# Wide product columns, turned gate rows, and a moved seam in two projection, attention and PLE stages

## The reference

```python
hn = rms_norm(h, g_mix[i])
z = hn @ w_in[i]                                   # 2840 columns
z_a, z_b, z_c = split_cols(z, (A_COLS, B_COLS, C_COLS))
y_a = chunked_spatial_gating(z_a, ...)             # 'mix': w @ layer_norm(v) + bias, times u
y_b = rwkv7_time_mix(z_b, ...)                     # a recurrence, 4 heads, 256 steps
y_c = nsa_attention(z_c, cos, sin, ...)            # three attentions, gates sigmoid(z)
h = h + jnp.concatenate([y_a, y_b, y_c], axis=-1) @ w_out[i]
h = h + (dense or expert FFN)(rms_norm(h, g_ffn[i]))
gate = jax.nn.sigmoid(rms_norm(h, g_ple[i]) @ ple_gate_w[i])
h = h + (p[i] @ ple_proj_w[i]) * gate
```

## Time and profile before

| | us |
|---|---|
| median of 3 runs | 2979.14 (2975.31 to 2981.68) |
| the profiled execution | 2979.76 |
| its span | 2978.0 |
| TensorE busy | 2824.9 (95%) |
| VectorE busy | 2056.7 (69%) |
| ScalarE busy | 1533.4 (51%) |
| projection, layer 0 | from 0.7 to 163.3 |
| attention, layer 0 | from 163.3 to 247 |
| PLE, layer 0 | from 437.9 to 478.8 |
| projection, layer 1 | from 478.9 to 629.2 |
| PLE, layer 1 | from 1568.5 to 1616.4 |

### The profile page before, as it was taken

How to read it: one execution, slowest core, us unless ns; L and a number is a source line. 1 busy time by engine, 2 the same in 40 slices (tenths; PEclk the granted TensorE clock), 3 DMA queues, 4 the chain that set the end, 5 groups by cost and what they waited for, 6 DMA issues and landing times. The chain is left out here.

```text
span 2978.0 us, 45722 instructions
## 1 busy us (share of the span) xinstructions
PE 2824.9 (95%) x17660; PEld 2382.1 (80%) x17660; DVE 2056.7 (69%) x2990; ACT 1533.4 (51%) x2398; POOL 21.4 (1%) x22
## 2 busy tenths in 40 slices
PE   8979999987999999999997999989999999989998
PEld 8847888954778777877786888979888888979887
DVE  7356764554888988898882776675576776675576
ACT  6144334233777777777773434554434434554433
POOL 0000000100000000000000000000000000000000
PEclk9999999997999999999998999999999999999999
DMA  6144543203788898898864556243554556244551
GB/s 264 48 168 147 194 154 118 97 1 134 294 330 340 333 363 331 335 366 337 339 248 183 204 194 207 80 162 145 183 193 146 204 194 203 84 160 146 184 195 38
DMA packets 102049, 599.07 MB, mean 201 GB/s; under 512 B 23166, under 2 KB 28798, under 8 KB 32780
## 3 DMA queue, kind: packets, MB, share of 16 engines
q1 hardware_dynamic: 101900, 596.99, 53.3%
HBM read 594.04 MB, written 6.12 MB: 202 GB/s over the span
## 5 line engine op out<-in xcount | busy, mean ns | idle before, releaser
L2393 DVE TENSOR_TENSOR expert_w_low<-weight_ring,expert_w_high 128x1024 fp32r<-128x1024 f32 x528 | 631.3, 1223 | 63.9 <-ACT expert_w_high L2337 53.4
L728 PE MATMUL psum<-hnT_parts,weight_high 128*128 128x512 f32 x1760 | 620.1, 394 | 0.5
L2337 ACT ACTIVATE expert_w_high<-weight_ring 128x1024 fp32r<-128x1024 f32 x528 | 555.2, 1059 | 100.4 <-PE psum L2268 56.8
L730 PE MATMUL psum<-hnT_parts,weight_low 128*128 128x256 f32 x1760 | 493.0, 280 | 0.0
L782 DVE TENSOR_TENSOR weight_low<-weight_ring,weight_high 128x1024 fp32r<-128x1024 f32 x330 | 384.8, 1219 | 12.0 <-ACT weight_high L776 12.0
L728 PEld LDWEIGHTS psum<-hnT_parts,weight_high 128*128 128x128 f32 x1760 | 330.8, 188 | 75.8 <-DVE hnT_parts L469 1.6
L730 PEld LDWEIGHTS psum<-hnT_parts,weight_low 128*128 128x128 f32 x1760 | 331.2, 188 | 3.9
L776 ACT ACTIVATE weight_high<-weight_ring 128x1024 fp32r<-128x1024 f32 x330 | 324.8, 1045 | 8.3 <-PE psum L747 8.3
L795 ACT ACTIVATE gate_act<-gate_sum 128x256 f32<-128x256 f32 x110 | 46.0, 418 | 519.5 <-DVE gate_sum L827 519.5
L2268 PE MATMUL psum<-expert_w_high,expert_x_high 128*128 128x512 f32 x704 | 288.5, 410 | 2.0 <-DVE expert_x_low L2412 1.9
L2268 PE MATMUL psum<-expert_w_high,expert_x_low 128*128 128x512 f32 x704 | 276.3, 392 | 0.0
(11 more groups left out here) (397 smaller groups left out, 4798.0 us busy)
## 6 DMA issues: line engine op xcount, KB each, us to landing
weight_ring<-in_moe_w SPq DMA_DIRECT2D x264, 1024.0 KB, 6.8
weight_ring<-in_w_in SPq DMA_DIRECT2D x52, 1024.0 KB, 5.5
weight_ring<-in_ffn_w_gate SPq DMA_DIRECT2D x44, 1024.0 KB, 4.8
weight_ring<-in_ffn_w_up SPq DMA_DIRECT2D x44, 1024.0 KB, 6.5
weight_ring<-in_ffn_w_down SPq DMA_DIRECT2D x44, 1024.0 KB, 4.7
weight_ring<-in_ffn_w SPq DMA_DIRECT2D x33, 1024.0 KB, 4.9
weight_ring<-in_w_gate SPq DMA_DIRECT2D x24, 1024.0 KB, 5.0
weight_ring<-in_w_branch SPq DMA_DIRECT2D x24, 512.0 KB, 3.4
```

What stands on the lines that cost most here:

```text
L728: nc.tensor.matmul(out, hi[:, kt, :], hn[2][:, kt, :, :], start=(kt == 0), stop=(kt == KT - 1), skip_group_check=True)
L730: last = nc.tensor.matmul(out[:, 0:SEQ], lo[:, kt, :], hn[0][:, kt, :], start=False, stop=(kt == KT - 1), skip_group_check=True)
L2337: nc.scalar.activation(part(0, k, half), raw(c, k, half), ACT.Copy).then_inc(high[k].sem, 1)
L2393: nc.vector.tensor_tensor(part(1, k, half), raw(c, k, half), as_f(part(0, k, half)), ALU.subtract).then_inc(low[k].sem, 1)
```

## The change

- `w_in`'s columns are relaid on the host: vs and kw change places. Slab 9 becomes ks and kw (job `keys`, both halves with 256 moving tokens), slab 10 becomes vs and vw (job `rows`, two token blocks with 256 moving columns). Both key tiles are stored by one ACT copy, both value tiles by one DVE copy.
- The gates job has its 24 weight columns stationary and 256 tokens moving; ACT applies the sigmoid to a 24 x 256 tile that lies in `kcT`, TensorE turns it (`turn_gates`, a new job `gate_rows`) and DVE copies it.
- The bias table's matmul stands between jobs u and v, its DVE operation behind `S.low(v, 6)`; `write_scratch` is issued behind the key tiles' moves as before.
- Of the eight compress parts three stand in the chunk loop behind part 0, and 4 to 7 behind it. `store("rope3")` moves into chunk 0 on DVE; its temporary tile is `gm_sq` instead of `Z`.
- The last four operations on Y move from the projection's end to the attention stage, behind `logits(0)`; the turn of Y moves behind the output products of s = 1 and its store to s = 2. `out_until` gives four products at s = 1 and one at each later step up to s = 25.
- `ple_stage` uses `product3` with split slabs and split hn; a slab's slot is released when it is split.

```diff
@@ -1113,22 +1118,13 @@
-                    if n in ("ks", "kw") and half == 0:
-                        parts = [(out[:, 0:SEQ], "w", slice(0, P))]
-                    elif n in ("ks", "kw"):
-                        parts = [(out[:, SEQ + b * P:SEQ + (b + 1) * P], b, slice(P, 2 * P)) for b in range(NBLK)]
-                    elif n == "v":
-                        parts = [(out[:, half * SEQ:(half + 1) * SEQ], half, slice(0, 256))]
-                    elif n == "gates":
-                        parts = [(out[:, half * 24:(half + 1) * 24], half, slice(0, 24))]
-                    else:
-                        parts = [(out[:, half * SEQ:(half + 1) * SEQ], "w", slice(half * P, (half + 1) * P))]
-                    for dst, left, cols in parts:
-                        tokens = slice(None) if left == "w" else slice(left * P, (left + 1) * P)
-                        steps = [([part[:, kt, cols] for part in w], [x[:, kt, tokens] for x in hn[0:2]]) for kt in range(KT)]
-                        last = product3(nc, dst, steps if left == "w" else [(x, y) for y, x in steps], ready)
-                        ready = None
-                    if half:
+                    by_row = n in ("v", "rows")
+                    cols = slice(0, 24) if n == "gates" else slice(0, 256) if by_row else slice(half * P, (half + 1) * P)
+                    tokens = slice(half * P, (half + 1) * P) if by_row else slice(None)
+                    dst = out[0:24, 0:SEQ] if n == "gates" else out[:, half * SEQ:(half + 1) * SEQ]
+                    steps = [([part[:, kt, cols] for part in w], [x[:, kt, tokens] for x in hn[0:2]]) for kt in range(KT)]
+                    last = product3(nc, dst, [(x, y) for y, x in steps] if by_row else steps, ready)
+                    if half or n == "gates":
@@ -1237,9 +1233,16 @@
+                def turn_gates():
+                    out = take_bank("gate_rows")
+                    t.wait_ge(*stored("gates"))
+                    for b in range(NBLK):
+                        last = nc.tensor.transpose(out[:, b * 24:(b + 1) * 24], gateT[:, b * P:(b + 1) * P], K.c("ident")[0:24, 0:24])
+                    last.then_inc(K.product.sem, 1)
@@ -1308,6 +1311,10 @@
+                    t.wait_ge(*dve("clamped"))
+                    mm(bank[4][0:12, :], T.table[:, :], K.c("bucket"), start=True, stop=True).then_inc(K.bias_step.sem, 1)
@@ -1365,24 +1374,18 @@
+                chunk_solve(1)
                 compress_part(2)
-                chunk_solve(1)
-                compress_part(3)
                 chunk_out(1)
                 chunk_rhs(2)
-                compress_part(4)
                 chunk_solve(2)
-                compress_part(5)
+                compress_part(3)
                 chunk_out(2)
                 chunk_rhs(3)
-                compress_part(6)
                 chunk_solve(3)
                 chunk_out(3)
-                compress_part(7)
-                if first_layer:
-
-                    t.wait_ge(*stored("rope2"))
-                    mm(bank_of("rope2")[0:12, :], T.table[:, :], K.c("bucket"), start=True, stop=True).then_inc(K.bias_step.sem, 1)
+                for k in range(4, 8):
+                    compress_part(k)
@@ -1681,6 +1690,8 @@
+                    if c == 0:
+                        store("rope3")
@@ -1704,16 +1715,6 @@
-                v.wait_ge(*pool("shift_ready"))
-                L(mult(Y, Y, scale[:, :, :]))
-                store("rope3")
-                v.wait_ge(*act("gn_root"))
-                L(nc.vector.reciprocal(stat[:, 0, :], stat[:, 2, :]))
-                L(mult(all_m(Y), all_m(Y), spread(stat[:, 0, :])))
-                nc.vector.tensor_tensor(Y, Y, shift[:, :, :], ALU.add)
-                if first_layer:
-                    v.wait_ge(*K.bias_step(1))
-                    nc.vector.tensor_tensor(T.bias_rows[:, :], bank_of("rope2")[0:12, :], K.c("rel_mask"), ALU.add).then_inc(K.bias_step.sem, 1)
@@ -1859,7 +1860,7 @@
-            return min(N_OUT - 4, 28 * s // (U + LEAD))
+            return min(3 + s, 8 if s < 4 else 16 if s < 9 else 20 if s < 15 else 24 if s < 21 else 28)
@@ -1930,20 +1941,15 @@
-                    for n in range(out_until(s - 1), out_until(s)):
+                    for n in range(out_until(s - 1) if s > 1 else 0, out_until(s)):
                         out_product(n)
+                    if s == 1:
+                        turn_y()
@@ -1979,7 +1985,14 @@
-                    if s == 1:
+                    if s == 0:
+                        stat = T.gn_stat
+                        all_m = lambda t: t.rearrange("p c (t d) -> p (c t) d", d=HD)
+                        L(nc.vector.tensor_tensor(Y, Y, T.y_scale[:, :, :], ALU.mult))
+                        L(nc.vector.reciprocal(stat[:, 0, :], stat[:, 2, :]))
+                        L(nc.vector.tensor_tensor(all_m(Y), all_m(Y), stat[:, 0, :].unsqueeze(2).broadcast_to([P, 2 * NRC, HD]), ALU.mult))
+                        nc.vector.tensor_tensor(Y, Y, T.y_shift[:, :, :], ALU.add).then_inc(*dve.mark("y"))
+                    if s == 2:
                         v.wait_ge(*pe("y_turned"))
                         nc.vector.tensor_copy(T.yT[:, 2:4, :], value_bank[:, :].rearrange("p (a b) -> p a b", b=SEQ)).then_inc(*dve.mark("yb"))
@@ -2483,7 +2499,7 @@
-                W.stream(sp, name, lambda n: pe(("gate", n if n < n_slabs - 1 else count - 1)) if n < n_slabs else pe(("proj", n_slabs - 1)))
+                W.stream(sp, name, lambda n: S.split(n) if n < n_slabs else pe(("proj", n_slabs - 1)))
@@ -2501,16 +2517,17 @@
-                    t.wait_ge(*W.arrived(first + n))
-                    w = W.slab(first + n, 256)
+                    arrived, w = S.ready(t, n), S.both(n)
+
+                    def ready(kt):
+                        arrived(kt)
+                        norm.ready(t, kt)
+                        if 1 <= kt <= 4:
+                            norm.turn(t, kt + 3)
+
                     for b in blocks:
-                        for kt in range(KT):
-                            if n == 0 and b == 0:
-                                norm.ready(t, kt)
-                            last = nc.tensor.matmul(K.bank[bank][:, rows(b)], K.hnT[:, kt, b * P:(b + 1) * P], w[:, kt, :],
-                                                    start=(kt == 0), stop=(kt == KT - 1))
-                            if n == 0 and b == 0 and kt + 4 < KT:
-                                norm.turn(t, kt + 4)
+                        steps = [([x[:, kt, b * P:(b + 1) * P] for x in hn[0:2]], [part[:, kt, :] for part in w]) for kt in range(KT)]
+                        last = product3(nc, K.bank[bank][:, rows(b)], steps, ready if n == 0 and b == 0 else None)
@@ -2531,8 +2548,10 @@
                 norm.root(a)
+                S.high(a, 0)
                 for kt in range(KT):
-                    norm.whole(a, kt)
+                    norm.high(a, kt)
+                S.high(a, 1)
@@ -3315,6 +3341,9 @@
+    w_in = np.array(inputs["w_in"])
+    w_in[:, :, KV_AT + P:KV_AT + 3 * P] = w_in[:, :, KV_AT + P:KV_AT + 3 * P].reshape(NLAYER, DM, 2, P)[:, :, ::-1].reshape(NLAYER, DM, 2 * P)
+    arrays["in_w_in"] = column_slabs(w_in)
```

104 lines of the change are left out of this document (65 added, 39 removed).

## The result

| | median us | range, runs |
|---|---|---|
| before | 2980.41 | 2975.31 to 2985.70, 4 |
| after | 2936.61 | 2934.88 to 2937.03, 4 |
| ratio | 0.9859 | 95% interval 0.9844 to 0.9874 |

Two of the twelve runs of the kernel before that stand beside e1 to e4 took 3435 and 3579 us at a lower mean granted clock (0.77 and 0.74 instead of 0.97) and are left out of every comparison.

A forecast was written before the change was run, and what follows sets the result against it. TensorE, busy 95% of the span, was taken to bound the kernel. Savings of 23.25 us in layer 0 and 22.05 in layer 1, together 45.3 off 2979.76, gave 2934.5 us; range 2924 to 2945.

The forecast's parts named there:

- Gates and clock: Projection's end: turned gates save 2.3 us a layer; half the time lost to low clock goes, 3.45 us.
- The bias row: Layer 0's projection: the matmul fills TensorE's wait before job v, but its DVE operation delays the split, +0.6 us.
- The seam, layer 0: Last Y product to first score: SP's bias-row transfers leave, the compress parts end the block; 5.6 us saved.
- Layer 1: Seam into layer 1's attention: 7.7 us becomes 6.4, 1.3 saved; less if compress parts ran at 1.2 GHz.
- Attention: Attention stage: later first probability costs 1.3 us, three fewer output products save 2.6; net 1.3 less per layer.
- PLE: PLE stage: three-part products save 5.0 us, waiting for slab 1's split loses 0.6; 4.4 less per layer.
- Behind PLE 1: After layer 1's PLE: slots freed by the split let the gain rows land earlier, 2.5 us less.
- rival F: Seams: another thing ends the blocks at the same times, 11 to 13 us less gain, 2947; chance 0.06.
- B: Projection's end: clock stays up through the mix job too, 2 x 3.45 us less, 2927.6; chance 0.13.
- C: Projection's end: clock dips as before, from the gates or four parts, 2 x 3.45 more, 2941.4; chance 0.12.
- D: PLE stage: splits late, slab 1 waited for whole, 3.6 us more per layer, 2941.7; chance 0.07.
- E: Attention stage: entered at 1.2 GHz and never recovering, +54 us in each layer, 3043; chance 0.03.

The follow-up runs named there:

- e1: Kernel before with only the relaid columns, the jobs keys and rows, and the turned gates; 2957.0 us, ratio 0.9926.
- e4: Changed kernel with the gates job narrow again (48 matmuls of 24 moving columns, no turn); 2954.5 us, ratio 0.9915.
- e9: e5 with the gates job narrow again, as in e4; 2934.0 us, ratio 0.9852.
- e5: Changed kernel without the mix job's one-row bias matmuls; DVE adds the bias from a spread table; 2923.5 us, ratio 0.9808.
- e10: Changed kernel with the mix job's bias matmuls given 128 rows instead of one, bias left out; 2921.9 us, ratio 0.9810.
- e2: Kernel before with only the bias row, compress parts, Y operations and turn moved, and the new out_until; 2969.1 us, ratio 0.9971.
- e8: Changed kernel with the PLE slabs' slots released by the gate matmuls again, not by the split; 2940.6 us, ratio 0.9869.
- e3: Kernel before with only the PLE stage changed: product3, split slabs and their earlier release; 2971.2 us, ratio 0.9968.
- e6: Changed kernel with another plan of output products in attention: three first, then two, one or none a step; 2945.5 us, ratio 0.9882.

## Why the prediction was right, step by step

- **The relaid columns**: 5.0 us a layer forecast; TensorE's lead over before grows by 4.98 across the two jobs in layer 0.
- **Gates and clock**: 2.3 + 3.45 = 5.75 a layer forecast, 5.3 in both. The job is 3.27, the turn 0.22; about half of the low time is left. The step "the first loses its place; the mix job keeps its dip" held for its reasons too: e4 and e9 bring the first back with the narrow gates alone, e5 and e10 remove the second with the one-row matmuls alone. What it did not see is that one-row matmuls are slow themselves.
- **The bias row**: 0.6 forecast, 0.57 measured (the job behind it starts 0.73 later, at 63.04 for 62.31, but the stage was 0.16 late already at its first own product). The matmul is taken up by the wait, which is 0.43 now; DVE's addition is not.
- **The chunk loop**: 1.8 forecast, 1.71 measured, in both layers; rope3 in chunk 0 delays nothing.
- **The seam, layer 0**: 5.6 forecast, 5.98 measured. The parts end the seam, as forecast. **Layer 1**: 1.3 forecast, 0.1 measured. The forecast named this case ("if the parts ran at 1.2 GHz") and gave it no weight; it came in layer 1 and not in layer 0. With the parts at full clock the gain is there: 1.6 in e2.
- **Attention**: 1.3 forecast each, 0.0 and 0.5 measured. The three products fewer give 2.4 us of the 2.6 forecast. The front costs 2.2 to 2.4 where 1.35 stood: the four products took 5.2 and 4.7 us from their first start to the turn, where 3.9 was reckoned with only the first of them at 1.2 GHz. This is the term that was mis-sized most against its size.
- **PLE**: 4.4 forecast, 4.2 in each layer. A slab step paces at 0.365 us, and the wait for slab 1's split is 0.20, not 0.6. In layer 0 another 1.1 us came from a low stretch behind PLE that was 3.4 us shorter.
- **Behind PLE 1**: 2.5 forecast, 2.25 measured, and e8 shows that the slots' release brings it.
- **Not forecast**: 1.7 us in the MoE stage, in which nothing is changed. The low stretches that lie over its start were 6.8 us shorter.

By the table, five stretches gave 4.4 us less than forecast together (most of it layer 1's seam and the two attention stages), and PLE 0 and the MoE stage gave 2.7 more. Both sides are for the most part the clock's place in time, and that they cancel is luck. e3 shows the size of that luck: 2.9 us per projection with the same code. A range some us wide on each side is the least such a forecast needs. One slip stands in it: rival F, priced at 2947, lies outside the stated range of 2924 to 2945.

Of the rivals, B (no dip at all) did not come, but e5 and e10 show what it takes. C (two dips as before) did not come either: e1 and e4 tie the first dip to the narrow job. The rule of the Trainium skill that stood beside B (TensorE: Matmul & The Clock Gate, "Why this matters for your kernels") says that TensorE keeps its full clock while it is busy without gaps, and it has the trace against it once more: from 114 to 121 TensorE was busy 7.00 of 7.00 us at a clock of 0.52, while e10 held 1.00 over 7.00 of 7.00 us from 105 to 112. D fell with the wait of 0.20 us for slab 1, F with the seams. E did not come: after the first steps the clock was 1.00 through the changed kernel's attention stage, from 178 to 233.

## What to carry to other kernels

A TensorE that is busy all the time can still run at half its clock, as here for most of 114 to 121. Look at the granted clock of each short stretch, find the instruction that stands where it falls, and try that job in another form. Here the 24-column job turned into one of 256 moving columns, and the one-row products given 128 rows or moved to DVE, won twice each: by their own time and by the clock. Before trusting a gain of 3 us, compare stages in which nothing changed; here they moved by up to 3 us through the clock alone. A gap filled with other work is won only where no second chain waits right behind it: count the chain (here DVE's variance, ACT's root, its table load) before moving the filler.

## What the runs showed of the hardware

- A product with one row stationary in turn with one of 128 rows: 0.72 us for four instructions of 128 columns. With 128 rows in both, 0.22 for four (e10). The mix job went from 6.9 us, partly at 1.2 GHz (5.8 in e8, at full clock), to 1.0 without the one-row products (e5).
- The clock fell inside a job of matmuls with 24 moving columns and 128 stationary (e9: 0.50 from 112 to 116) and not with 24 stationary and 256 moving, which held 1.00 (104 to 108 of the changed kernel).
- The same instructions, begun 0.2 us apart, had a mean clock of 0.77 and 0.69 over 30 us (the kernel before and e3).
- In layer 0's attention, with TensorE busy 31 of 35 us in both, the clock was 1.00 with one product in each step and 0.85 with products two by two (changed kernel and e6). In layer 1 it stayed at 1.00 with products two by two as well, so the cause is open.
